# Decoder step on one core: the index stage loads x already turned and applies the row factors behind the projections

## The chip, the cores and the metric

One Trainium2 chip, one core. The metric is the device time of one execution in microseconds, as the median of several runs. Engines are named as in the profile: PE is TensorE, DVE VectorE, ACT ScalarE, POOL GpSimd, SP SyncE. A queue such as SPq or ACTq is that engine's issue of transfers.

## The reference, cut to what matters

Layer 0 of a two-layer decoder is sparse attention with an indexer. 1024 prompt rows and 64 sample rows (8 sequences of 8 tokens) of width 1024 are normed and projected; the indexer's queries (8 heads of 64), its one key per row (64) and its 8 head weights are part of that projection.

```python
def _rms_norm(x, gain):
    y = xf * lax.rsqrt(jnp.mean(xf * xf, axis=-1, keepdims=True) + EPS)
    return (y * gain).astype(x.dtype)

# _att_project, from xn = _rms_norm(x, att_norm)
q, k, v, iq, ik, iw, gate = _split(xn @ w_in, ATT_SIZES)
ik = _rms_norm(ik, ik_gain)
iw = iw * (IDX_HEADS ** -0.5 * IDX_DIM ** -0.5)

# _indexer_topk
s = jnp.einsum('bthd,bld->bthl', iq, ik)
score = jnp.einsum('bth,bthl->btl', iw, jax.nn.relu(s))
score = jnp.where(admissible, score, -jnp.inf)
_, idx = lax.top_k(score, topk)          # topk = 256
```

For the prompt the keys are the prompt's own; for the sample they are 8192 cached keys and the 8 new ones. A row factor r = rsqrt(mean(x^2) + EPS) multiplies a whole row of x, so it can be taken out of a product: x @ w with the gain alone gives iq / r, ik / r and iw / r. ReLU lets a positive factor through, so the score needs iw times r^2. The norm of ik cancels r but for its EPS: it becomes rsqrt(mean(ik_raw^2) + EPS * (mean(x^2) + EPS)).

## The kernel before, in words

`build` runs stages one after the other, each a block that all engines leave together: `index_project` (L217), `sample_scores` (L606), `head_project`, the attention of the prompt, and then the sample's attention and the DeltaNet layer. The change touches the first two and the tile `xnT` that they leave to the rest. Everything is float32.

**Rows and tiles.** Nine row tiles of 128 rows: tile 0 holds the 64 sample rows, tiles 1 to 8 the prompt. `xnT` is x normed and turned: 128 partitions of the width, 8 slices of it, 64 + 1024 columns of rows. Tiles are worked in three trios.

**`index_project`.** SP loads row tiles into a ring of three (`x`), the gain as a broadcast tile `gx`, key weights `wk` (72 columns) and query weights `wq` (512 columns). For each tile ScalarE sums the squares (L451), GpSimd forms the row factor (`rms_x`: L342, L343), VectorE multiplies row, factor and gain (`norm_x`, L519), TensorE turns the tile in 8 transposes (`transposes_x`, L373), and ScalarE copies them out (`evac_x`, L458). Then `keys(n)` (L383) projects the tile to 64 key and 8 head weight columns. ScalarE takes them (`take_keys`: L464, L465, squares in L471), GpSimd forms the key's factor (`rms_ik`: L350, L351), VectorE norms the key (`norm_ik`, L527), TensorE turns it (`transpose_ik`, L392) and ScalarE copies it to `ikT` (L477, L478). `queries(r)` (L407) projects a trio's queries in four parts, which ScalarE copies out (`take_queries`, L485).

TensorE's order is: transposes and keys of trio 0, its queries, its key transposes, the page ids (L433); then the same for trio 1 and the scores of prompt blocks 2 to 4; then for trio 2 and the scores of blocks 5 to 7. `key_scores` (L418) is followed by ScalarE's ReLU of two heads at a time (`relus`, L493, two buffers) and VectorE's weighted sum (`add_parts`, L540 and L544). GpSimd gathers eight pages of sample keys at the end of its list (`gather_keys`, L600), after all factors.

**The search.** The threshold of the top 256 of a prompt row is found bit by bit (`prompt_topk`): each step counts the scores above a candidate for each block of a group (L118, which also writes its accumulator), and then settles the bit in two small operations, L135 and L137, each waiting for the one before. At a group's end `choose` marks the chosen keys (L144 to L151). The first group (blocks 2 and 3) has 32 steps and 2 choices, the second (blocks 4 to 7) 32 and 4. `TOPK_IN` tells which steps lie in which stage: four after the first scores, eleven between `norm_ik(7)` and `norm_ik(8)`, 29 in `sample_scores`.

**`sample_scores`.** 32 gathers of 128 pages of 16 keys go through a ring of eight; each is used in two steps of TensorE. Gather n + 8 is released by the second use of gather n, so GpSimd has a burst of eight and then a pause. TensorE turns the keys (L679), multiplies (L689) and sums the heads (L702); ScalarE copies and applies ReLU (L736, L743). VectorE waits for a small mask (`cmn`), runs 29 search steps, and adds the mask to the last columns at the end (L766).

## Time and profile before

| | |
|---|---|
| median of 3 runs | 1866.98 us (1861.58 to 1869.72) |
| span of the profiled execution | 1911.6 us, 26707 instructions |
| that execution's own time around its span | not shown by the page |
| PE, DVE, ACT, POOL busy | 91%, 67%, 40%, 27% of the span |
| mean granted TensorE clock | 0.966 |
| mean over the span, DMA | 207.37 MB, 108 GB/s |
| index stage | 0 to 165 us |
| sample scores | 165 to 258 us |

The page gives busy time by engine and by line, for one execution; a time in the trace is counted from the first instruction. A row of the timeline has its start, its length, engine, line, operation, output and inputs, and in brackets how long the engine was idle before it and what released it.

### The profile page before, as it was taken

To read this page: it belongs to the slowest core of one execution; us is meant where nothing else is said; L and a number is where in the kernel's file an instruction comes from. 1 tells how busy PE (TensorE), PEld (TensorE's weight loads), DVE (VectorE), ACT (ScalarE), POOL (GpSimd) and SP (SyncE) were. 2 spreads that over 40 slices of the span, in tenths; PEclk is the share of its full clock that TensorE was granted. 3 is DMA by queue.
4 is the path that set the end of the run, shared out by engine and by line. 5 is a ranking of instruction groups with operands and counts; after the bars stand their busy time and mean duration, and the time that the engine had idled before them with its cause. 6 is when DMAs were issued, how large, how long until landed. Compare 5 with 4: busy or idle time off the path is not lost. (4 is left out here: it accounts for less than half of the span.)

```text
span 1911.6 us, 26707 instructions
## 1 busy us (share of the span) xinstructions
PE 1733.9 (91%) x10053; PEld 994.6 (52%) x10053; DVE 1274.5 (67%) x2068; ACT 759.6 (40%) x1805; POOL 518.8 (27%) x588
## 2 busy tenths in 40 slices
PE   6888999999989999999989769989996878999997
PEld 5453444444445566664434334434434776777774
DVE  1389957899976799964885334535553576777671
ACT  3447778852224344322212222222211544655550
POOL 2121300100101111002117666767522502222320
PEclk9999999999999999999999979999998899999999
DMA  4125530110124112003215445445579445343220
GB/s 132 36 91 174 180 135 14 44 39 28 56 111 176 66 67 101 32 12 136 67 44 145 123 122 154 147 143 157 149 266 325 119 130 141 109 105 87 76 63 36
DMA packets 159447, 207.37 MB, mean 108 GB/s; under 512 B 45160, under 2 KB 109120, under 8 KB 159296
## 3 DMA queue, kind: packets, MB, share of 16 engines
q1 hardware_dynamic: 117336, 149.65, 23.7%
q0 software_dynamic: 16896, 50.35, 8.7%
q10 hardware_dynamic: 25088, 5.66, 1.5%
q8 instruction: 81, 1.33, 0.3%
q14 instruction: 46, 0.38, 0.1%
HBM read 161.89 MB, written 43.74 MB: 108 GB/s over the span
## 5 line engine op out<-in xcount | busy, mean ns | idle before, releaser
L930 PE MATMUL acc<-w_qg,xnT 128*128 128x512 f32 x384 | 169.1, 593 | 0.0
L2130 POOL DMA_INDIRECT home<-in_cache_v,rowidx x128 | 129.6, 1013 | 68.7 <-issue 35.7
L1147 DVE MAX8 top_v<-scores 128x8 f32<-128x4100 f32 x32 | 141.6, 4426 | 0.3
L1149 DVE FIND_INDEX8 top_i<-top_v,scores 128x8 uint32<-128x4100 f32 x32 | 141.5, 4423 | 0.0
L1151 DVE MATCH_REPLACE8 scores<-top_v,scores 128x4100 f32<-128x4100 f32 x32 | 141.2, 4413 | 0.0
L3450 PE MATMUL PY<-home,ogT_dn 128*128 128x512 f32 x288 | 133.6, 609 | 5.8 <-DVE y_t L3936 5.1
L1348 PE MATMUL ring<-w_out_att,ogT_blk 128*128 128x512 f32 x256 | 111.4, 593 | 2.8 <-DMA w_out_att<-in_att_w_out 1.7
L930 PEld LDWEIGHTS acc<-w_qg,xnT 128*128 128x128 f32 x384 | 71.1, 190 | 81.6 <-issue 81.5
L930 PE MATMUL acc<-w_kvq,xnT 128*128 128x512 f32 x256 | 111.4, 593 | 0.0
L2453 DVE SCALAR_TENSOR_TENSOR y_ch<-x_pad,conv_w,y_ch 128x1024 f32<-128x1024 f32 x72 | 92.5, 1285 | 2.6
L186 ACT ACTIVATE junk_topk_h<-key_mask,bs_cand 128x640 f32<-128x640 f32 (+1 forms) x88 | 86.1, 981 | 15.7 <-DVE bs_cand L196 10.8
L1381 ACT COPY pT_blk<-tp_blk 128x512 f32<-128x512 f32 (+3 forms) x96 | 43.2, 487 | 123.6 <-PE tp_blk L1318 123.4
L2374 ACT COPY scores<-tpk 128x512 f32<-128x512 f32 x64 | 37.0, 588 | 137.1 <-PE tpk L2176 81.5
L2267 PE MATMUL acc_ch<-xnT,S_s 128*128 128x512 f32 x176 | 86.4, 636 | 4.1 <-issue 3.9
L2267 PE MATMUL acc_ch<-xnT,weight_sums 128*128 128x512 f32 x176 | 82.9, 614 | 4.1 <-issue 4.0
L3450 PEld LDWEIGHTS PY<-home,ogT_dn 128*128 128x128 f32 x288 | 53.3, 195 | 62.2 <-issue 60.8
L1309 PE MATMUL ring<-kT,w_kvq 128*128 128x512 f32 (+3 forms) x192 | 74.5, 499 | 11.9 <-DVE w_kvq L1454 5.6
L1429 DVE CUSTOM_DVE_ANT_0 lm<-ring,key_mask,q_scale 128x128 f32<-128x128 f32 (+7 forms) x64 | 51.7, 814 | 47.9 <-PE ring L1309 47.3
L1348 PEld LDWEIGHTS ring<-w_out_att,ogT_blk 128*128 128x128 f32 x256 | 48.3, 190 | 62.6 <-issue 61.0
L930 PEld LDWEIGHTS acc<-w_kvq,xnT 128*128 128x128 f32 x256 | 48.5, 190 | 61.1 <-issue 61.1
L2267 PE MATMUL acc_ch<-w_out_s,weight_sums 128*128 128x512 f32 x176 | 79.4, 594 | 0.3 <-issue 0.3
L1277 POOL TENSOR_TENSOR w_kvq<-w_kvq 128x512 f32<-128x512 f32 x15 | 19.1, 1276 | 216.6 <-ACT w_kvq L1394 215.6
(535 smaller groups left out, 3586.0 us busy)
## 6 DMA issues: line engine op xcount, KB each, us to landing
S_s<-in_dn_w_in SPq DMA_DIRECT2D x24, 512.0 KB
qkv_d<-y_ch SPq DMA_DIRECT2D x24, 512.0 KB
qkv_t<-qkv_d SPq DMA_DIRECT2D x8, 1536.0 KB, 8.1
home<-in_dn_w_in SPq DMA_DIRECT2D x5, 2048.0 KB, 11.2
x<-in_x_all SPq DMA_DIRECT2D x9, 512.0 KB, 3.7
out_y_all<-y_t SPq DMA_DIRECT2D x9, 512.0 KB, 2.9
w_kvq<-in_att_w_in SPq DMA_DIRECT2D x2, 2048.0 KB, 7.8
w_qg<-in_att_w_in SPq DMA_DIRECT2D x2, 2048.0 KB, 12.6
```

The lines of the kernel that those rows point to most:

```text
L186: ins = act.activation(self.junk[:, a:a + w], self.block(i), ACT.Sign, bias=self.cand[:, s:s + 1].bitcast(F32), scale=-1.0, accum_out=self ...
L930: ins = pe.matmul(acc[rows(n), k % ACC, :], xnT[:, kk, cols(n)], w[:, kk, :], start=(kk == 0), stop=(kk == KT - 1))
L1147: link(dve.max(v, scores[:]))
L1149: dve.max_index(top_i[:, 8 * r:8 * r + 8], v, scores[:])
L1151: link(dve.match_replace(scores[:], v, scores[:], -3e38))
L1309: ins = pe.matmul(dst[:, a:a + w], q[:, i % 2, h, :], kT[:, h // GRP, a:a + w], start=True, stop=True)
L1348: ins = pe.matmul(dst[:, a:a + 512], ogT[:, h, :], wo[:, h, a:a + 512], start=(h == 0), stop=(h == H - 1))
L1429: dve.tensor_tensor_reduce(lm[:, hc % LR, 0:w], ring[:, at["l", hc] % 2, 0:w], key_mask[:, KM[i]:KM[i] + w], keep["q_scale"][:, i, h:h + 1 ...
L2130: pool.indirect_dma_start(vg[:, j % VR, c, :], None, cv, bass.IndirectOffsetOnAxis(ap=rowidx[:, c, query(j):query(j) + 1], axis=0)).then_i ...
L2267: ins = pe.matmul(dst, left[:, k, :], right[:, k, :], start=(first and k == 0), stop=(last and k == 3), skip_group_check=True)
L2453: ins = dve.scalar_tensor_tensor(out, src, tap, out, ALU.mult, ALU.add)
L3450: ins = pe.matmul(PY[:], ogT[:, h, :], wo[:, h, r * 512:(r + 1) * 512], start=(h == 0), stop=(h == H - 1))
```

## The change

- The host hands in `x_cols`, x turned, and the gain by columns. SP loads it by trios straight into `xnT`, the first trio in two halves, and the query weights in two halves; VectorE multiplies slices of a trio by the gain in place (`gains`). Transposes, norms and evictions of x are gone.
- The row tiles are still loaded, by ScalarE's queue, three at once at the start, only for the sum of squares.
- GpSimd forms the row factor, its square and EPS times the mean for each tile, and multiplies the head weights (`rms_x`, `rms_ik`). Key tiles have three buffers instead of two.
- TensorE: keys 0 and 1, queries 0, keys 2 to 5, key transposes 0 to 2, page ids, queries 1, keys 6 to 8, key transposes 3 to 5, early scores, queries 2, key transposes 6 to 8, late scores. GpSimd gathers between the factors of tile 5 and those of tile 6. VectorE norms keys 3 to 8 ahead of the early sums.
- The search runs 13 steps in the index stage, all between early and late sums, and 31 in the sample scores.
- The row factors go to DRAM and come back as a broadcast row of 1088 to all partitions, the first load of the sample scores; there GpSimd multiplies the eight slices of `xnT` by it, one behind every third gather.

```diff
-TOPK_IN = {"index": (0, 4), "index_late": (4, 15), "sample_scores": (15, 44), "heads": (34 + 32, len(SEARCH))}
+TOPK_IN = {"index": (0, 13), "sample_scores": (13, 44), "heads": (34 + 32, len(SEARCH))}
...
 # SP, index_project
+            sp.dma_start(xnT[:, 0:4, trio(0)], xv[:, 0:4, trio(0)]).then_inc(xt_in[0], 16)
+            sp.dma_start(gxc[:], d["att_norm_cols"]).then_inc(gxc_in, 16)
+            sp.dma_start(wk[:], wv[:, :, IK0:G0]).then_inc(wk_in, 16)
+            sp.dma_start(xnT[:, 4:8, trio(0)], xv[:, 4:8, trio(0)]).then_inc(xt_in[1], 16)
+            sp.dma_start(wq[:, :, 0:256], wv[:, :, IQ0:IQ0 + 256]).then_inc(wq_in[0], 16)
+            sp.dma_start(wq[:, :, 256:512], wv[:, :, IQ0 + 256:IK0]).then_inc(wq_in[1], 16)
             sp.dma_start(ident[:], d["c_ident"]).then_inc(const_in, 16)
+            sp.dma_start(xnT[:, :, trio(1)], xv[:, :, trio(1)]).then_inc(xt_in[2], 16)
...
+            sp.dma_start(xnT[:, :, trio(2)], xv[:, :, trio(2)]).then_inc(xt_in[3], 16)
+            sp.wait_ge(rsi_ok, 1)
...
+            sp.wait_ge(rsx_ok, NT)
+                sp.dma_start(d["rs_d"][:, 0:NS].rearrange("o p -> p o"), rsx[0:NS, 0, :]).then_inc(rs_out, 16)
+                sp.dma_start(d["rs_d"][:, NS:].rearrange("o (n p) -> p (o n)", p=P), rsx[:, 1:NT, :].rearrange("p n o -> p (n o)")).then_inc(rs_out, 16)
...
 # GpSimd
             def rms_x(n):
                 pool.wait_ge(ssx_ok, n + 1)
+                link(pool.tensor_scalar(msx[:, n, :], ssx[:, n, :], 1.0 / DM, EPS, ALU.mult, ALU.add))
+                pool.tensor_scalar(epsm[:, n, :], msx[:, n, :], EPS, None, ALU.mult)
+                link(pool.tensor_tensor(rsx[:, n, :], msx[:, n, :], mhalf[:], ALU.pow))
+                link(pool.tensor_tensor(rs2[:, n, :], rsx[:, n, :], rsx[:, n, :], ALU.mult))
+                pool.tensor_scalar(rs2[:, n, :], rs2[:, n, :], IH ** -0.5 * ID ** -0.5, None, ALU.mult).then_inc(rsx_ok, 1)
             def rms_ik(n):
+                pool.wait_ge(rsx_ok, n + 1)
+                pool.tensor_scalar(iw_nat[q, n, :], ikr[q, n % 3, ID:ID + IH], rs2[q, n, :], None, ALU.mult)
+                link(pool.tensor_scalar(msi[q, n, :], ssi[q, n, :], 1.0 / ID, None, ALU.mult))
+                link(pool.tensor_tensor(msi[q, n, :], msi[q, n, :], epsm[q, n, :], ALU.add))
+                pool.tensor_tensor(rsi[q, n, :], msi[q, n, :], mhalf[q, :], ALU.pow).then_inc(rsi_ok, 1)
...
+            for n in range(3, 6):
+                rms_x(n)
+                rms_ik(n)
             pool.wait_ge(idx_ok, 1)
             gather_keys(pool, d, keep, k_in, 0, RING)
+            for n in range(6, NT):
+                rms_x(n)
+                rms_ik(n)
...
 # TensorE
+            keys(0)
+            keys(1)
+            queries(0)
+            for n in range(2, 6):
+                keys(n)
+            for n in range(3):
+                transpose_ik(n)
...
 # ScalarE
+                act.activation(junk[:], x[:, n % XR, :], ACT.Square, accum_out=ssx[:, n, :]).then_inc(ssx_ok, 1)
+                if n + XR < NT:
+                    act.wait_ge(ssx_ok, n + 1)
+                    load(n + XR)
...
+            for n in range(XR):
+                load(n)
+            take_keys(0)
+            take_keys(1)
+            for g in range(4):
+                take_queries(0, g)
+                if g < 3:
+                    square_x(g)
...
 # VectorE
+            def gains(r):
+                    dve.tensor_scalar(xnT[:, k, trio(r)], xnT[:, k, trio(r)], gxc[:, k:k + 1], None, ALU.mult).then_inc(xg_ok, 1)
...
+            for n in range(3, NT):
+                norm_ik(n)
+            for i in EARLY:
+                add_parts(i)
+            topk(*TOPK_IN["index"])
+            for i in LATE:
+                add_parts(i)
...
 # sample_scores
         def _(sp):
+            sp.wait_ge(env["stores"]["rs_out"], 32)
+            sp.dma_start(keep["rs_row"][:], d["rs_d"].partition_broadcast(P)).then_inc(rs_in, 16)
             sp.dma_start(cmn[:], d["c_new_causal"]).then_inc(loads, 16)
...
                 gather_keys(pool, d, keep, k_in, n, n + 1)
+                if n % 3 == 2:
+                    k = (n - RING) // 3
+                    if k == 0:
+                        pool.wait_ge(rs_in, 16)
+                    pool.tensor_tensor(xnT[:, k, :], xnT[:, k, :], keep["rs_row"][:], ALU.mult)
```

## Rows read from the trace of the kernel before

**Rows 1.** Busy time by stretch: span and length; engines with counts; clock; DMA share; GB/s.

```profile
46.60:60.50 13.90, 9.51 (x77) 8.57 (x77) 6.86 (x22) 7.56 (x21) 3.18 (x6) 1.00 0.27 82
60.50:81.00 20.50, 20.50 (x67) 12.15 (x66) 1.68 (x3) 3.62 (x13) 3.65 (x7) 1.00 0.08 27
...
83.50:105.20 21.70, 16.00 (x80) 6.69 (x81) 18.55 (x36) 13.98 (x19) 0.00 (x0) 1.00 0.00 0
...
111.30:134.40 23.10, 21.50 (x70) 12.57 (x69) 19.73 (x76) 4.00 (x14) 8.65 (x11) 1.00 0.53 187
134.40:165.00 30.60, 23.84 (x96) 7.40 (x96) 28.47 (x51) 21.80 (x24) 0.00 (x0) 0.98 0.00 0
165.00:258.00 93.00, 85.32 (x688) 38.65 (x688) 81.39 (x218) 71.66 (x105) 23.52 (x24) 0.97 0.53 182
```

The engines in each row are PE, its weight loads, DVE, ACT and POOL.

**Rows 2.** Timeline of the index stage.

```profile
7.16 1.28 DVE L519 SCALAR_TENSOR_TENSOR x<-x,rsx,gx 128x1024 f32<-128x1024 f32 x1 [7.16 <-DMA gx<-in_att_norm_rows]
...
21.68 1.06 ACT L451 ACTIVATE junk_x<-x 128x1024 f32<-128x1024 f32 x1 [5.52 <-DMA x<-in_x_all]
...
24.37 3.69 PE L383 MATMUL ik_ps<-w_ik,xnT 128*128 128x72 f32 x16 [5.26 <-ACT xnT L458]
...
27.85 18.69 PE L407 MATMUL iq_key_score<-xnT,w_iq 128*128 128x320 f32 x64
...
103.06 0.70 ACT L493 ACTIVATE relu_parts<-iq_key_score 128x640 f32<-128x640 f32 x1 [0.22 <-DVE key_mask L544]
```

**Rows 3.** Timeline of DVE in the sample scores.

```profile
167.01 0.61 DVE L118 TENSOR_SCALAR_CACHE_REDUCE junk_topk_s<-key_mask,bs_cand 128x384 f32<-128x384 f32 x1 [2.13 <-DMA new_causal<-in_c_new_causal]
...
195.98 0.17 DVE L135 TENSOR_SCALAR bs_rej<-bs_cnt 128x2 int32<-128x2 f32 x1
...
196.38 0.61 DVE L118 TENSOR_SCALAR_CACHE_REDUCE junk_topk_s<-key_mask,bs_cand 128x384 f32<-128x384 f32 x1
...
205.07 0.82 DVE L118 TENSOR_SCALAR_CACHE_REDUCE junk_topk_s<-key_mask 128x640 f32<-128x640 f32 x1
...
251.64 0.16 DVE L137 SCALAR_TENSOR_TENSOR bs_cand<-bs_cand,bs_rej 128x4 int32<-128x4 int32 x1
...
257.44 0.16 DVE L766 TENSOR_TENSOR scores<-rps,new_causal 128x4 f32<-128x4 f32 x1 [5.64 <-PE rps L727]
```

**Rows 4.** DMA totals from 12 to 20 us.

```profile
DMA packets 2197, 2.79 MB, mean 349 GB/s; under 512 B 880, under 2 KB 1024, under 8 KB 2197
```

**Rows 5.** Lines of the index stage, shapes apart: busy us, mean ns | idle.

```profile
L383 PE MATMUL ik_ps<-w_ik,xnT 128*128 128x72 f32 x128 | 17.0, 292 | 5.7 <-ACT xnT L458 5.7
...
L351 POOL TENSOR_TENSOR rsi<-msi,mhalf 128x1 f32<-128x1 f32 x8 | 4.3, 544 | 0.7
...
L350 POOL TENSOR_SCALAR msi<-ssi 128x1 f32<-128x1 f32 x8 | 1.5, 192 | 53.4 <-ACT junk_ik L471 53.2
...
L540 DVE TENSOR_SCALAR key_mask<-relu_parts,iw_nat 128x320 f32<-128x320 f32 x2 | 0.7, 384 | 0.0
```

**Rows 6.** Busy time in stretches of 2 us around the first queries (granted clock third last).

```profile
24.00:26.00 2.00, 1.63 (x8) 1.63 (x8) 1.67 (x3) 0.32 (x1) 1.92 (x2) 0.50 0.00 0
...
30.00:32.00 2.00, 2.00 (x8) 1.44 (x7) 0.46 (x3) 1.09 (x9) 1.06 (x4) 0.91 0.00 0
```

**Rows 7.** Timeline where DVE and POOL meet: a later stage, and the sample scores.

```profile
222.61 0.94 POOL L600 DMA_INDIRECT kraw<-in_cache_idx_k,idx_page  x1 [0.30 <-issue]
223.15 0.39 DVE L135 TENSOR_SCALAR bs_rej<-bs_cnt 128x4 int32<-128x4 f32 x1
...
888.14 2.34 POOL L1638 TENSOR_TENSOR gz<-tanh_z,gain_o 128x1024 f32<-128x1024 f32 x1
888.28 3.29 DVE L1817 SCALAR_TENSOR_TENSOR dn_ahead<-dn_ahead,dn_rs 128x1024 f32<-128x1024 f32 x1 [0.52 <-POOL dn_rs L1632]
```

**Rows 8.** Timeline of POOL in the sample scores: the first gathers of two bursts.

```profile
176.72 0.94 POOL L600 DMA_INDIRECT kraw<-in_cache_idx_k,idx_page  x1 [52.50 <-PE tps L679]
...
198.51 1.56 POOL L600 DMA_INDIRECT kraw<-in_cache_idx_k,idx_page  x1 [10.98 <-PE tps L679]
```

More of the change, by code:

```diff
@@ new lines, in _ @@
+            keys(1)
+            queries(0)
+            for n in range(2, 6):
+                keys(n)
+            for n in range(3):
+                transpose_ik(n)
+            pe.wait_ge(ptf_ok, 1)
+            pe.matmul(kq[:, 2, 0:DB * NGI], e16[:], ptf[:], start=True, stop=True).then_inc(ptb_ok, 1)
+            queries(1)
+            for n in range(6, NT):
+                keys(n)
+            for n in range(3, 6):
+                transpose_ik(n)
+            pe.wait_ge(idx_ok, 1)
+            pe.wait_ge(iq_ok, 8)
@@ L442, in _, with load @@
+            pe.wait_ge(tp_evac, 6)
+            for i in EARLY:
+                key_scores(i)
+            queries(2)
+            for n in range(6, NT):
+                transpose_ik(n)
+            pe.wait_ge(iq_ok, 12)
+            pe.wait_ge(tp_evac, NT)
+            pe.wait_ge(zeroed, 1)
+            for i in LATE:
+                key_scores(i)
         @block.scalar
         def _(act):
+            def load(n):
+                act.dma_start(x[:, n % XR, :], d["x_all"][n * P:(n + 1) * P, :]).then_inc(x_in[n % XR], 16)
@@ L473, in evac_ik @@
             def evac_ik(n):
[L474 removed]
                 m = NS if n == 0 else P
[L476 to L485 removed]
+                act.wait_ge(tp_done, n + 1)
```

323 lines of the change are left out of this document (125 added, 198 removed).

## The prediction

> **What bounds the kernel now.** TensorE is busy for 91% of the span, but the change touches only the first 258 us, so I read those by stage [rows 1]. The index stage ends at 165 us and is a relay. Until 27.85 us TensorE waits for rows: the first norm starts when the broadcast gain has landed at 7.16, ScalarE stands until 21.68 for a row tile, so the third keys run at 24.37 and the first queries at 27.85 [rows 2]. From 46.6 to 60.5 it turns and projects three more tiles. From 83.5 to 105.2 and from 134.4 to 165 the score sums bound: VectorE is busy for 18.55 of 21.7 us and 28.47 of 30.6 [rows 1]. Between these, TensorE turns and projects the last trio until 111.3, and the third queries hide VectorE's search (19.73 busy of 23.1). The sample scores (165 to 258) hold TensorE for 85.32 of 93 us and VectorE for 81.39 [rows 1]. There TensorE ends last: VectorE's last search step ends soon after 251.64, and it idles for 5.64 us before its last sum at 257.44 [rows 3]. These 5.6 us are all the slack it has, and the forecast turns on them.
>
> The stages end at common borders: a stage is worth what its last engine says, and the next keeps what it gains. The profiled span is 1911.6 us, and no time of that execution around its span is shown; the median of the runs, 1866.98, is 2.3% less. I take the difference from the profile and put it on the median.
>
> **The change, part by part: index stage.** *Opening.* Gone: the gain rows (512 KB), the transposes, norms and evictions of x. Needed before the first queries: two halves of the turned trio (655 KB each), key weights (295 KB) and half of the query weights (1 MB), and beside them on ScalarE's queue three row tiles (1.5 MB) that nothing early needs: 4.2 MB. Full queues moved 2.79 MB in 8 us, 349 GB/s [rows 4]; 4.2 MB are then 12.1 us, and with the first bytes at 2 us and about 1 us to the semaphore the query weights land at 15. The second half of the trio, with all ahead of it (3.2 MB), lands near 12; its four gain multiplications, of the form of the score sum's first product, 384 ns at 320 columns [rows 5], end near 13.5. Keys of two tiles follow: eight tiles took 17.0 us, 2.1 each [rows 5], more at low clock: keys began at a granted clock of 0.50 (1.2 of 2.4 GHz) after TensorE had stood for 5.26 us [rows 2, 6]. I take the first queries at 17: minus 10.9 us. Bounds: 15, weights just landed and keys quick; 21, at 250 GB/s. Of the first queries a part ran at half clock until about 31 [rows 6]; now TensorE runs without a hole before them: minus 1.2 (nothing to 1.5).
>
> *Between first and second queries.* Before 13.9 us [rows 1]. After: keys of four tiles (7.6 to 8.4 by rows 5) and small transposes with the page ids (1.7, an estimate from the 2.5 between the second queries and 83.5): 9.3. Minus 4.6.
>
> *Around the early scores.* The last rectified block ends at 103.8 [rows 2], the third queries began at 111.3: 7.5 us now go, but the keys of that trio come back ahead of the early scores, 5.8. Minus 1.7.
>
> *GpSimd's queue, a new wait.* VectorE now norms all nine key tiles before its first score sum, and the last three need row factors that GpSimd forms only after eight gathers. With second queries from 43.8 and 5.2 us for each of their four parts, the sixth tile's squares end at 56 and its factors at 59; eight gathers of 0.94 us with 0.3 between [rows 8] last until 69; three tiles of nine small operations each, 192 ns or for the powers 544 ns [rows 5] with 80 ns between, and the norm, until 78.4. The sums could have begun at 74.6: the second queries' end, 64.7, the keys and 4.1 of small steps. ScalarE and TensorE hold two buffers each and queue behind. Plus 3.8 (nothing to 6).
>
> *At nothing.* The search: 13 steps, not 15, are now all beside the third queries: 22.5 us at 1.73 each (rows 3, below) against 23.1 of cover [rows 1]; a step more would show whole. The squares of the row tiles (1.06 us, rows 2) lie between evictions 5 us apart; the six later loads cost ScalarE some 0.5 us of issue there. Later gains: beside queries. SP's ten head weight transfers now wait for the first key factor (about 26) and are needed near 50. SP's store of 1,088 row factors leaves near 78 and is wanted at 150; the last key stores stand behind it, and no one waits for them. Were that cover gone, each is 2 to 3 us.
>
> Sum for the stage: -10.9 -1.2 -4.6 -1.7 +3.8 = **-14.6**; it ends near 150.4.
>
> **Sample scores.** Three things go onto VectorE. (1) The row factors' broadcast (557 KB) is issued ahead of the small mask load for which VectorE waits until 167.01 [rows 3]: at 349 GB/s plus 1.5. (2) Two search steps: 17 took from 167.01 to 196.38, 1.73 each: plus 3.45. (3) Eight multiplications of 128x1088 on GpSimd, one after every third gather. The nearest row is 2.34 us for 128x1024 [rows 7], so 2.5 us each. They hold VectorE up: an operation with two inputs in SBUF that takes 1.28 us at 7.16 [rows 2] took 3.29 when it began 0.14 us behind such a multiplication, and ended 1.09 us after it [rows 7]. The search's small operation L135 took 0.39 us, not 0.17, and ended with a gather [rows 3, 7]. Every search step has a pair of such small operations, L135 and L137; the long counts have one tensor input, and no row shows them held.
>
> So each multiplication stops the search at its next small pair. In the first group (steps of 1.73) it is met after 0.86 us on average and holds for 2.5 - 0.86 = 1.64. In the second (10 steps from 205.07 to 251.64, 4.66 each) it is met in 2.5/4.66 of cases and holds for 1.25: 0.67. Gathers start at 176.72 and 198.51 [rows 8], 11.5 and 33.3 us into the stage, and three with a multiplication take 6.4 us. So four fall in the first group (6.6), two in the choosing between the groups (8.7 us, nearly all two-input or short operations; 1.7 and 2.3), two in the second group (1.3): 11.9, less 0.5 where waits overlap. 1.5 + 3.45 + 11.4 - 5.6 of slack = **+10.8**. Bounds: nothing if they never hold it (4.95 is under the slack), and with 8 times 2.5 for 11.4, +19.4, if the counts are held too. I take the middle: rows 7 show small and two-input operations held and nothing else.
>
> The Trainium skill says (SBUF — State Buffer, Who interferes with whom) that the shared port pair is taken for a whole instruction, and that the form of tensor_scalar that also writes its accumulator stays outside. By that exemption the stage's sum is +10.8, without it +19.4; no row here decides it for a long multiplication beside a long count.
>
> Gathers 9 to 15 go out later, behind three multiplications; TensorE may be 1 us late, but has 9 until VectorE ends. What shows instead is the clock: TensorE stands for 10 us before the projections. After 5.26 us of standing it had half clock from 24.37 to about 31 [rows 2, 6], 3 us lost; I take half, plus 1.5 (nothing to 3).
>
> **Sum:** -14.6 + 10.8 + 1.5 = -2.3. Predicted 1864.7.
>
> **The rivals.** *A, the lock hides.* If GpSimd gives way, or its work falls beside counts, VectorE ends within its slack, and the stage grows by 2 at most. For it: most of a step is a count. Against it: 3.29 us [rows 7]. Time: -14.6 + 2 = -12.6, 1854.4. *B, a shorter relay.* The factors fit (no 3.8) and the weights land at once: index -19.5, net -7, 1860. *C, slower: the opening is bound by its loads.* Place: the query weights' first half. The turned rows come in pieces of 1280 bytes, and the row tiles take every second turn on the other queue. Price: at half the rate of rows 4, 175 GB/s, 4.2 MB are 24 us; first queries at 27 as before, -14.6 becomes -4.6: net +8, 1875. It decides from where the weights land after 24 us. Against it: 349 GB/s were moved with small pieces among them. That the change doesn't do what it says would be the same place: turned loads as late as the transposes.
>
> **How the numbers follow.** Forecast 0.55 (its own range 1857 to 1872), A 0.17, B 0.16, C 0.12. A measurement can tell about 0.5% (9.3 us) from no change. Beyond it lie most of A (0.13), a quarter of B (0.04) and the forecast's tail (0.02): faster 0.19. Half of C (0.06) and the forecast with held counts (0.03): slower 0.09. Same 0.72. The range, 1853 to 1876, reaches from A to C and leaves under 0.2 out.
>
> **What would show it.** First queries near 17 us; only keys and small transposes between first and second queries; VectorE's first score sum some 4 us after it could start, released by a key factor; the border near 150. Then L135 or L137 up to 2.5 us long beside GpSimd's multiplications, and TensorE, not VectorE, idle at the end of the sample scores. I am wrong if VectorE still idles there for microseconds (A), or if the first queries wait for weights beyond 21 us (C).

## The result, and the profile after

Beside each other on one chip the changed kernel takes 1877.63 us (median of 6 runs, 1871.19 to 1884.37) and the kernel before 1864.98 (6 runs, 1861.58 to 1869.72): a ratio of 1.0070, 95% interval 1.0051 to 1.0089. A second set gave 1.0066 (1.0042 to 1.0090). The change costs 12.7 us where a gain of 2.3 was forecast, and the result lies outside the range of 1853 to 1876. (Runs taken beside each other are a set. "Set 1860.76" behind a time below is the median of the kernel before in the same set.)

| | before | after |
|---|---|---|
| median | 1864.98 us | 1877.63 us |
| profiled execution, its span | 1911.6 | 1875.8 (its own time 1877.61) |
| TensorE's first queries | 27.85 | 17.12 |
| index stage ends (VectorE's last operation in it) | 164.9 | 153.3 |
| VectorE's last sum of the sample scores | 257.4 | 264.0 |
| first product of the heads | 258.3 | 264.9 |

The span of before, 1911.6, is no contradiction. In some sets both kernels take some 60 us more, nearly all between 1040 and 1300 us, and what makes it is not known: one chip has a set of each kind (1923.07 and 1863.32 us for the kernel before). So times are compared only with those of the kernel before in the same set, and profiles by stretches that end at the same instructions.

The opening, in the timeline of TensorE, answers to [rows 2] (start, length, engine, line, in brackets the idle time before and what ended it):

```profile
10.09 1.22 PE L373 MATMUL ik_ps<-w_ik,xnT 128*64 128x72 f32 x8 [10.09 <-DMA w_ik<-in_att_w_in]
12.31 5.01 PE L373 MATMUL ik_ps<-w_ik,xnT 128*64 128x72 f32 x24 [1.00 <-DVE xnT L526]
17.12 18.82 PE L397 MATMUL iq_key_score<-xnT,w_iq 128*128 128x320 f32 x64
35.78 7.26 PE L373 MATMUL ik_ps<-w_ik,xnT 128*128 128x72 f32 x64
...
44.69 5.75 PE L397 MATMUL iq_key_score<-xnT,w_iq 128*128 128x384 f32 x17
```

First queries at 17.12, and 8.8 us between the end of the first (35.94) and the second (44.69): close to the forecast, 17 and 9.3. The queries took 18.82 us, as before (18.69), so the 1.2 us for the clock were not there: in both kernels the first four products start 0.53 to 0.63 us apart, and the later ones 0.27. The timeline of VectorE around the early scores:

```profile
73.95 0.48 DVE L534 SCALAR_TENSOR_TENSOR ikk<-ik_raw,rsi,gik 128x64 f32<-128x64 f32 x2 [13.12 <-POOL rsi L349]
77.52 0.48 DVE L534 SCALAR_TENSOR_TENSOR ikk<-ik_raw,rsi,gik 128x64 f32<-128x64 f32 x2 [3.09 <-POOL rsi L349]
81.08 0.48 DVE L534 SCALAR_TENSOR_TENSOR ikk<-ik_raw,rsi,gik 128x64 f32<-128x64 f32 x2 [3.08 <-POOL rsi L349]
81.48 0.41 DVE L547 TENSOR_SCALAR key_mask<-relu_parts,iw_nat 128x384 f32<-128x384 f32 x1
```

The new wait is there, the three last norms behind GpSimd's factors. They come 3.57 us apart, where nine operations at the forecast's prices are 3.15, and the first sum starts at 81.5, not 78.4.

In the sample scores VectorE now ends last. Its timeline (answers to [rows 3]), and GpSimd's at two of these places:

```profile
158.69 0.61 DVE L118 TENSOR_SCALAR_CACHE_REDUCE junk_topk_s<-key_mask,bs_cand 128x384 f32<-128x384 f32 x1 [5.45 <-DMA new_causal<-in_c_new_causal]
...
166.90 2.38 DVE L135 TENSOR_SCALAR bs_rej<-bs_cnt 128x2 int32<-128x2 f32 x1
...
172.56 2.89 DVE L135 TENSOR_SCALAR bs_rej<-bs_cnt 128x2 int32<-128x2 f32 x1
...
178.72 2.87 DVE L135 TENSOR_SCALAR bs_rej<-bs_cnt 128x2 int32<-128x2 f32 x1
...
264.03 0.16 DVE L776 TENSOR_TENSOR scores<-rps,new_causal 128x4 f32<-128x4 f32 x1
```

```profile
171.95 0.94 POOL L603 DMA_INDIRECT kraw<-in_cache_idx_k,idx_page  x1 [0.30 <-issue]
172.91 2.50 POOL L678 TENSOR_TENSOR xnT<-xnT,rs_row 128x1088 f32<-128x1088 f32 x1
175.57 0.98 POOL L603 DMA_INDIRECT kraw<-in_cache_idx_k,idx_page  x1 [0.16 <-PE tps L689]
...
178.09 0.94 POOL L603 DMA_INDIRECT kraw<-in_cache_idx_k,idx_page  x1 [0.30 <-issue]
179.05 2.50 POOL L678 TENSOR_TENSOR xnT<-xnT,rs_row 128x1088 f32<-128x1088 f32 x1
```

L135 starts at 172.56, inside the gather, and ends at 175.45, in the gap of 0.16 us behind the multiplication. Time that an operation takes beyond its own, because GpSimd is at work, is called a hold here. There are eight, six of 2.2 to 2.8 us and two of 0.5 and 1.5, in all 17.8 us above the 0.17 that such an operation takes alone. TensorE waits too, for gathers that leave late. Its waits for gathers from 153.4 to 251 us (total, times, longest), and the busy times there and from 251 to 264.9 (answer to [rows 1]):

```profile
PE tps L689 <- DMA kraw<-in_cache_idx_k,idx_page: 6.8, 8, 2.2
```

```profile
153.40:251.00 97.60, 88.30 (x688) 38.97 (x688) 88.92 (x202) 73.10 (x105) 43.03 (x32) 0.95 0.53 179
251.00:264.90 13.90, 0.02 (x2) 0.05 (x2) 12.78 (x29) 0.00 (x0) 0.21 (x5) 0.54 0.00 0
```

(Columns: stretch, its length, busy us of TensorE's matmuls and weight loads, VectorE, ScalarE, GpSimd, the granted clock, DMA share, GB/s.) In the last 13.9 us VectorE works alone.

### The profile page after: what moved, and what is told of

Same layout as the page of the kernel before. It is cut to its first block and busy times, and to the rows that moved or that the text cites. A ratio compares the mean times of both kernels' runs of the same rounds, so it can differ in the third digit from the quotient of the medians.

```text
span 1875.8 us, 26591 instructions
## 1 busy us (share of the span) xinstructions
PE 1722.0 (92%) x9981; PEld 986.5 (53%) x9981; DVE 1288.2 (69%) x2083; ACT 752.0 (40%) x1778; POOL 545.8 (29%) x641
## 5 line engine op out<-in xcount | busy, mean ns | idle before, releaser
L940 PEld LDWEIGHTS acc<-w_qg,xnT 128*128 128x128 f32 x384 | 71.1, 190 | 81.6 <-issue 81.5
L186 ACT ACTIVATE junk_topk_h<-key_mask,bs_cand 128x640 f32<-128x640 f32 (+1 forms) x88 | 86.1, 981 | 29.0 <-issue 18.4
L1319 PE MATMUL ring<-kT,w_kvq 128*128 128x512 f32 (+3 forms) x192 | 75.0, 502 | 12.5 <-PEq L784 6.1
L1287 POOL TENSOR_TENSOR w_kvq<-w_kvq 128x512 f32<-128x512 f32 x15 | 19.1, 1275 | 217.7 <-ACT w_kvq L1404 216.7
L2277 PE MATMUL acc_ch<-xnT,S_s 128*128 128x512 f32 x176 | 81.9, 609 | 0.0
## 6 DMA issues: line engine op xcount, KB each, us to landing
home<-in_dn_w_in SPq DMA_DIRECT2D x5, 2048.0 KB, 10.9
```

The lines of the kernel that those rows point to most:

```text
L186: ins = act.activation(self.junk[:, a:a + w], self.block(i), ACT.Sign, bias=self.cand[:, s:s + 1].bitcast(F32), scale=-1.0, accum_out=self ...
L940: ins = pe.matmul(acc[rows(n), k % ACC, :], xnT[:, kk, cols(n)], w[:, kk, :], start=(kk == 0), stop=(kk == KT - 1))
L1319: ins = pe.matmul(dst[:, a:a + w], q[:, i % 2, h, :], kT[:, h // GRP, a:a + w], start=True, stop=True)
L2277: ins = pe.matmul(dst, left[:, k, :], right[:, k, :], start=(first and k == 0), stop=(last and k == 3), skip_group_check=True)
```

## The experiments

**The kernel before again, twice, and the changed kernel again, twice.** No edit. The forecast rests on one profile of before.

> The kernel before once more, for a second profile of it. The profiled execution that stands in the front part took 1911.6 us of span against 1866.98 us of the median; aligned by instruction, it loses some 45 us between 1040 and 1300 us and nothing before. Expected: a span within 0.5% of 1865 us, and up to 280 us the same times as the first profile within 1 us (index stage ends at 164.9, VectorE's last addition of the sample scores at 257.4).

> The changed kernel once more, for a second profile and a tighter time. Against the second profile of the kernel before, its first profile stands 6.9 us behind at 280 us, 8.7 at 600, 9.2 at 1100, and 17.5 to 18.8 from 1560 us to the end. If the last 8 us are a cost of the change, the second profile has them too; if they are the state of TensorE's clock where the scan begins, the two profiles differ there by several us. Expected: 6.5 to 7.5 us behind at 280 us, as the holds of VectorE repeat, and a time 9 to 15 us above the kernel before.

> The kernel before once more, beside the changed one on the same chip, for the stretch behind 1440 us. If the changed kernel loses there by its order or its streams, this profile runs level with the other profiles of the kernel before (within 2 us of each other from 1440 to 1850) and the changed kernel's falls behind it by 6 us or more; if it is the clock's chance, this one falls behind its own kind by as much.

> The changed kernel on the same chip as the profile of the kernel before beside it. By the theory of the holds it stands 5 to 8 us behind at 280 us; by the losses seen so far 7 to 10 us behind at 1000 us; and if the loss behind 1440 us belongs to the change, 6 us more at the end.

| profile | index stage ends | VectorE's last sum | heads' first product | holds |
|---|---|---|---|---|
| before, first | 164.9 | 257.4 | 258.3 | 0.5 |
| before, second (e0) | 170.3 | 257.0 | 257.8 | 0.4 |
| before, third (e11) | 170.7 | 262.3 | 263.1 | 0.4 |
| after, first | 153.3 | 264.0 | 264.9 | 17.8 |
| after, second (e7) | 153.5 | 261.5 | 262.4 | 15.5 |
| after, third (e12) | 153.5 | 261.9 | 262.7 | 15.5 |

The expectation of e0 was missed: the kernel before varies by 6 us in the index stage and by 5 at the heads, the changed one by 0.2 and 2.5. The index stage varies with TensorE's clock. From 54.6 to 68.3 us, in the first profile of before, in e0 and in the first profile of the changed kernel (columns as above, the granted clock third last):

```profile
54.60:68.30 13.70, 12.38 (x64) 9.14 (x65) 3.35 (x6) 6.48 (x23) 6.28 (x11) 1.00 0.18 59
```

```profile
54.60:68.30 13.70, 13.13 (x48) 11.04 (x49) 3.35 (x6) 5.71 (x20) 6.77 (x12) 0.50 0.15 49
```

```profile
54.60:68.30 13.70, 13.70 (x62) 9.20 (x60) 1.02 (x5) 4.42 (x11) 9.21 (x17) 1.00 0.60 171
```

In e0 TensorE ran at half clock for the second trio's products and into its queries, and the third queries began at 116.81 instead of 111.42. e11 has the same (0.52), the changed kernel's profiles do not (1.00 in all three). VectorE's slack varies too. The 5.64 us of the first profile are 5.06 in e11 and nothing in e0, where TensorE ended at 256.58 and the last sum follows VectorE's own last step:

```profile
256.96 0.16 DVE L766 TENSOR_TENSOR scores<-rps,new_causal 128x4 f32<-128x4 f32 x1
```

In the mean the changed kernel starts the heads at 263.3, the kernel before at 259.7: 3.6 us of the 12.7 are lost by then. The time of e7 was as expected (9 to 15 us above), but at 280 us it stood 4.9 us behind e0, not 6.5 to 7.5. The expectation of e12 was missed: beside e11 it was 0.7 us ahead at 280 us, 0.3 behind at 1000 and 1.9 behind at the end. That of e11 was missed in part. Its scan is level with its own kind (the stretches below), but from 1700 to 1850 us it lost 8.6 us against e0, 7.3 of them behind 1780, where its clock was granted 0.50 twice for 6.8 us. That hides the scan's 8.5 us between e11 and e12 at the end. The times of e0, 1859.41 us (set 1860.76), and of e11 and e12, 1930.57 and 1932.33 (set 1923.07), are single runs.

**Without the multiplications (e1).** The projections of the heads then lack the row factor of x.

```diff
-                if n % 3 == 2:
...
-                    pool.tensor_tensor(xnT[:, k, :], xnT[:, k, :], keep["rs_row"][:], ALU.mult)
```

> The changed kernel without GpSimd's eight multiplications of 2.50 us (it leaves out the row factor of x for the projections of the heads). Theory (the multiplications hold VectorE's search: eight waits of 0.64 to 2.99 us, 15.8 us in all): the waits go, VectorE's last addition of the sample scores comes at 247 to 250 us instead of 264.0, with TensorE's scores as the bound or level with it, and the time falls by 13 to 17 us, to 1861 to 1865 us. Rival (the two search steps more and the late mask load are what costs, and the holds are noise in a search that waits anyhow): the addition stays at 260 us or later and the time within 5 us of 1877.6.

The last sum is at 246.4, with no hold, and the ratio to before is 0.9983 (0.9962 to 1.0003), 16 us under the changed kernel. TensorE's part of the sample scores fell from 97.0 us to 86.8, its 6.8 us of waits for gathers gone; the rest is no more than that part varies by (91.9, 85.8 and 90.9 us in the three profiles of before). TensorE ended at 240.6, so VectorE still set the end, where the expectation had the two level. Its chain from the index stage's end to the last sum is 93.2 us against 86.7 in e0, which is the late mask and the two steps. So the eight multiplications are most of what made the stage long, on both engines.

**All eight behind the last gather (e4).**

```diff
-                if n % 3 == 2:
-                    k = (n - RING) // 3
-                    if k == 0:
-                        pool.wait_ge(rs_in, 16)
-                    pool.tensor_tensor(xnT[:, k, :], xnT[:, k, :], keep["rs_row"][:], ALU.mult)
+            pool.wait_ge(rs_in, 16)
+            for k in range(KT):
+                pool.tensor_tensor(xnT[:, k, :], xnT[:, k, :], keep["rs_row"][:], ALU.mult)
```

> The changed kernel with all eight multiplications behind the last gather instead of one behind every third. Theory (each hold is the alignment of one short operation of the search with a gather and the multiplication right behind it, 15.8 us in all; and every multiplication delays the next gathers, for which TensorE waits 6.8 us): in a row, each multiplication of 2.5 us stretches one search step of 1.72 us to 2.5 us, 8 x 0.8 = 6.4 us and up to 2.5 us for the first, so 7 to 9 us instead of 15.8, TensorE ends 4 to 6 us earlier than at 250.8, and VectorE's last addition comes 7 to 9 us earlier than 264.0; the time falls by 6 to 9 us. Rival (the multiplications take a fixed toll of the search, 2 us each, wherever they stand): VectorE's waits stay at 14 to 17 us and the addition within 2 us of 264.0.

The ratio is 1.0074 (1.0046 to 1.0102): no gain. TensorE ended at 241.3, 9 us earlier, where the theory had 4 to 6. But VectorE's last sum stayed at 264.5; there the rival had the size, by another mechanism. The timelines of VectorE and GpSimd:

```profile
217.61 1.28 DVE L118 TENSOR_SCALAR_CACHE_REDUCE junk_topk_s<-key_mask,bs_cand 128x1024 f32<-128x1024 f32 x1
218.93 17.43 DVE L135 TENSOR_SCALAR bs_rej<-bs_cnt 128x4 int32<-128x4 f32 x1
236.40 0.16 DVE L137 SCALAR_TENSOR_TENSOR bs_cand<-bs_cand,bs_rej 128x4 int32<-128x4 int32 x1
```

```profile
216.64 19.70 POOL L676 TENSOR_TENSOR xnT<-xnT,rs_row 128x1088 f32<-128x1088 f32 x8
```

One hold of 17.4 us, which ends when GpSimd's row does, at 236.34. Between multiplications that follow without a gap VectorE's operation doesn't get in. The theory had given it a turn behind each.

**The same multiplications, paced (e10).** GpSimd begins each when the search's chain has counted the end of a step: two tiles in halves, beside steps of the first group (1.4 us of counts), six whole, beside steps of the second (4.3 us).

```diff
+        PACED = {15: [(i // 2, halves[i % 2], first + 3 * (13 + i)) for i in range(4)],
+                 23: [(2 + i, whole, pairs + 4 * (1 + i)) for i in range(2)],
+                 31: [(4 + i, whole, pairs + 4 * (6 + i)) for i in range(4)]}
...
+                    pool.wait_ge(env["topk_chain"]["sem"], done)
+                    pool.tensor_tensor(xnT[:, k, part], xnT[:, k, part], keep["rs_row"][:, part], ALU.mult)
```

> The changed kernel with the same eight multiplications on GpSimd, but each begun when the search's chain says that a step has just ended: four halves of 544 columns behind gather 16, two whole ones behind gather 24, four behind the last gather (two tiles as halves, six whole). Theory (what holds VectorE is one short operation of the search arriving inside an unbroken run of GpSimd work, until that run ends; it is not the multiplications' share of time, nor their number): a whole one of 2.5 us fits into the 4.3 us of long operations of a step of the second group, a half one of 1.25 us into the 1.4 us of the first group, so the holds fall from 15.5 to 17.8 us to under 4, VectorE's last addition comes at 247 to 251 us instead of 261.6 to 264.2, and the time is 10 to 15 us less than the changed kernel's, ratio to the kernel before 0.997 to 1.001. Rival (GpSimd's multiplications take their time from VectorE wherever they fall): the holds show up in the long operations or behind them, and the addition stays at 260 us or later.

GpSimd, and VectorE beside it:

```profile
205.66 2.52 POOL L683 TENSOR_TENSOR xnT<-xnT,rs_row 128x1088 f32<-128x1088 f32 x1 [5.61 <-DVE bs_cand L131]
```

```profile
205.62 0.88 DVE L118 TENSOR_SCALAR_CACHE_REDUCE junk_topk_s<-key_mask,bs_cand 128x640 f32<-128x640 f32 x1
206.42 1.01 DVE L118 TENSOR_SCALAR_CACHE_REDUCE junk_topk_s<-key_mask,bs_cand 128x768 f32<-128x768 f32 x1
207.35 1.14 DVE L118 TENSOR_SCALAR_CACHE_REDUCE junk_topk_s<-key_mask,bs_cand 128x896 f32<-128x896 f32 x1
208.54 1.28 DVE L118 TENSOR_SCALAR_CACHE_REDUCE junk_topk_s<-key_mask,bs_cand 128x1024 f32<-128x1024 f32 x1
209.86 0.17 DVE L135 TENSOR_SCALAR bs_rej<-bs_cnt 128x4 int32<-128x4 f32 x1
...
248.97 0.16 DVE L781 TENSOR_TENSOR scores<-rps,new_causal 128x4 f32<-128x4 f32 x1 [1.56 <-PE rps L742]
```

All the arithmetic is there, and no operation of the search is held by more than 0.3 us. The counts beside a multiplication are as long (0.88, 1.01) as those of the next step without one. The last sum, at 249.0, waits for TensorE again. The ratio is 0.9995 (0.9970 to 1.0021). This shows the mechanism: not the load, but a short operation that arrives inside an unbroken run of GpSimd's work.

**Three small parts (e2, e3, e6), one run each.** The first asks for the mask ahead of the row factors.

```diff
+            sp.dma_start(cmn[:], d["c_new_causal"]).then_inc(loads, 16)
             sp.wait_ge(env["stores"]["rs_out"], 32)
             sp.dma_start(keep["rs_row"][:], d["rs_d"].partition_broadcast(P)).then_inc(rs_in, 16)
-            sp.dma_start(cmn[:], d["c_new_causal"]).then_inc(loads, 16)
```

> The changed kernel with the load of the 4-column mask asked for ahead of the row factors' load (544 KB to all partitions) and of the wait for the factors' store. Theory: VectorE's search starts 3 to 4 us earlier (it began at 158.7 with a wait of 5.45 us for that load), and as VectorE sets the end of the sample scores, its last addition comes 2 to 4 us earlier than 264.0, unless the shift brings more of the search's short operations under GpSimd's multiplications (1 to 2 us either way). Rival (TensorE sets the end of the stage): the addition stays at 264.0 within 1 us and shows idle time behind TensorE.

The search starts 2.9 us into the stage instead of 5.5, and the last sum is at 262.5 (1872.30 us; set 1860.76). The late mask costs about 2.5 us, of which holds of 18.0 us left little. The second puts the gathers behind the last factors.

```diff
-            pool.wait_ge(idx_ok, 1)
-            gather_keys(pool, d, keep, k_in, 0, RING)
             for n in range(6, NT):
                 rms_x(n)
                 rms_ik(n)
+            pool.wait_ge(idx_ok, 1)
+            gather_keys(pool, d, keep, k_in, 0, RING)
```

> The changed kernel with GpSimd's first eight gathers behind the factors of the last three tiles instead of ahead of them. Theory: the factors of tiles 6 to 8, which come at 73.9, 77.5 and 81.1 us behind gathers that end at 70.4, come 10 us earlier, VectorE begins the early sums at 74 to 76 us instead of 81.5, the early scores end 5 to 6 us earlier, and the index stage ends at 147 to 149 us instead of 153.7; the gathers still land long before the sample scores. Rival (TensorE or ScalarE hold the early scores then): the stage ends less than 2 us earlier.

The first early sum starts at 78.0 and the index stage ends at 150.3: 3 us earlier, not 5 to 6. VectorE still waits for factors: with the gathers out of the way GpSimd waits 6.93 us for ScalarE's squares of tile 6. Most of the 3 us is gone by the last sum (261.7; 1932.37 us, set 1922.99): the holds come to 18.4. The third moves two search steps back.

```diff
-TOPK_IN = {"index": (0, 13), "sample_scores": (13, 44), ...
+TOPK_IN = {"index": (0, 15), "sample_scores": (15, 44), ...
```

> The changed kernel with 15 search steps in the index stage and 29 in the sample scores, as the kernel before has it, instead of 13 and 31. Theory: two steps of 1.72 us leave the sample scores, where VectorE sets the end, and enter the index stage, where VectorE waits for TensorE by less than that: the index stage ends 2 to 3.5 us later, the sample scores take 3.5 us less, and the sum is within 1.5 us of no change, up to one hold of 2.7 us either way. Rival (the move of the two steps is what made the sample scores longer): VectorE's last addition comes 3 us or more earlier than 264.0.

The index stage ends 2.4 us later (155.8), the last sum is at 262.9 (1938.63 us, set 1928.02). Moving the two steps is a wash.

**Natural rows later (e5).**

```diff
-            for n in range(XR):
-                load(n)
             take_keys(0)
             take_keys(1)
+            for n in range(XR):
+                load(n)
```

> The changed kernel with ScalarE's three first loads of rows in natural layout (512 KB each) asked for behind its copies of the first two tiles' keys instead of at once. Theory: in the opening 2.8 MB of rows, turned x and weights share the DMA engines at some 350 GB/s; without 1.5 MB of rows ahead of them the second half of x, the key weights and the query weights land 3 to 4 us earlier, the first queries begin at 13 to 14 us instead of 17.1, and all up to the end of the early scores follows by as much, unless the squares of the rows then come too late for the norms of tiles 0 to 2. Rival (the opening waits for its own loads' latency): the first queries begin within 1 us of 17.1.

First queries at 13.5, 3.7 us earlier than in e7; the index stage ends at 150.4. The rows were in the way of the opening, as expected. At the last sum 0.7 us is left (260.8), with holds of 17.8. Its time, 1923.47 us (set 1928.02), is a single run and lower than its stretches account for.

**The row factor in ScalarE's copies (f1), and without its scratch tensor (f1b).** ScalarE scales by the row's factor where it copies the heads' projections out; the multiplications, the factors' store and broadcast go. Not in the lines shown: the sample rows are loaded twice, so that their factors stand in both halves of the partitions.

```diff
-                    act.copy(v_nat[q, n, :], src[:, 256:512])
+                    act.mul(v_nat[q, n, :], src[:, 256:512], f)
...
-                act.activation(sgate[:, 0, 0:512], acc[:, k % ACC, :], ACT.Silu).then_inc(acc_rd, 1)
+                act.activation(sgate[:, 0, 0:512], acc[:, k % ACC, :], ACT.Silu, scale=keep["rsx"][:, 0, :]).then_inc(acc_rd, 1)
```

> The changed kernel with the row factor of x taken into ScalarE's copies out of PSUM in the projections of the heads (scale by the row's factor), instead of GpSimd's eight multiplications; the factors' store and the load to all partitions go too. Theory: the search is held by nothing and the mask no longer waits behind 544 KB, so VectorE's last addition comes 3 to 4 us earlier than in the kernel without multiplications (246.4), at 242 to 244 us, and the time is 2 to 5 us less than that kernel's 1858.4, so 8 to 3 us below the kernel before. Rival (ScalarE's copies with a scale by the row take longer, and ScalarE is what the projections wait for): the gain at 247 us is given back by 530 us.

> The same as the kernel with the factor in the copies, with the scratch tensor of the row factors (4352 bytes in DRAM, unused there) taken out, so that every DRAM tensor behind it lies where it lay before. All changed kernels lose 7 to 9 us against the kernel before between 1440 and 1850 us, where the code is the same and short transfers to and from DRAM stand in the chain. Theory (their addresses matter): this kernel is 4 to 8 us faster than the one with the tensor, all of it behind 1440 us. Rival (the clock's dips fall otherwise): the two are within 2 us.

Ratios 0.9982 (0.9962 to 1.0002) and 0.9982 (0.9960 to 1.0004). The last sum is at 249.5 and 248.0, not 242 to 244, and TensorE sets it again. Two things made it later: the index stage ended at 158.0 and 156.0, with first queries at 18.7 and 18.9 (probably the second load of the sample rows, which nothing tests), and TensorE's part took 90.8 and 91.3 us instead of e1's 86.8. The scratch tensor's place in DRAM made no difference to the time, so DRAM addresses are out as the cause of the later loss.

**All of it (f3): factor in the copies, gathers last, rows late.**

> The kernel with the row factor in ScalarE's copies, with the first eight gathers behind the factors of tiles 6 to 8 (3 us earlier early sums in the run that has this alone), and with the natural rows asked for behind the first keys. Theory: the gains add, as TensorE now sets the end of the sample scores and its start follows the index stage: the index stage ends at 147 to 149 us, the sample scores at 240 to 243, and the time is 5 to 7 us below that of the kernel with the factor in the copies alone, ratio to the kernel before 0.993 to 0.996. Rival (the first gathers, now later, or the rows, now later, take their place): ratio within 0.001 of 0.998.

The ratio is **0.9924** (0.9896 to 0.9952), faster than both kernels. The index stage ends at 147.9, the heads begin at 240.3. Freed of the holds, both small parts keep their gain.

**72 transposes more on TensorE (f4 from f3, e13 from the changed kernel), and 36 and 144 (e14, e15 from f3).**

```diff
+            pe.wait_ge(const_in, 16)
+            for _ in range(72):
+                pe.transpose(tpb[0:32, 0, 3, 0:32], ident[0:32, 0:32], ident[0:32, 0:32])
             for n in range(3):
                 transpose_ik(n)
```

> The same kernel with 72 more transposes of 32 x 32 on TensorE (their output is not used), placed where TensorE waits for the norms of tiles 0 to 2: it makes TensorE's instruction stream as long as that of the kernel before, which had 72 transposes of x. All changed kernels lose 6 to 9 us against the kernel before between 1440 and 1850 us in code that is the same; in each of them TensorE's queue stands for 2.4 to 3.1 us without a wait at the second group of products of the state (u with k_masked) at 1507 to 1529 us, where the kernel before has 1.6 us or none. Theory (where the stream lies relative to its loading decides): that stall is gone here and the kernel is 2 to 5 us faster than its twin behind 1440 us. Rival: the stall stays and the two lie within 2 us.

> The changed kernel as it is, with 72 transposes of 32 x 32 on TensorE more (output unused) where TensorE waits for the norms of tiles 0 to 2; they took 2.3 us there. Four profiles of changed kernels at a time show the same in the stretch of the scan that the three profiles of the kernel before pass in 139.8 to 140.2 us (1560 to 1700): 142.8 to 147.7 us, with 2.9 to 6.0 us in 4 or 5 stalls of TensorE without a wait against 0.3 to 0.6 us in one; and 61 to 67 us against 59.9 to 60.7 in the 60 us ahead of it. The one kernel with 72 transposes added has 140.1 and 60.7 us and one stall. Theory (taking 72 transposes out of TensorE's stream shifted where its loading falls in the scan's code): here too 60 to 61 us and 140 to 141 us, and a time 4 to 8 us below the changed kernel's, ratio to the kernel before 1.002 to 1.005. Rival (what the one kernel showed was chance, or its other edits): 143 to 146 us and the ratio at 1.0066 to 1.0074.

> The kernel with the factor in the copies, the gathers last and the rows late (its scan stretches: 64.1 and 142.8 us), with 36 transposes added instead of 72. If the position of the stream decides, the stalls fall on other instructions than with none or with 72: the two stretches come out between 200 and 209 us in sum, by where they fall, and the lines with stalls differ from those of both. If each added transpose helps by itself, the sum lies midway, at 203 to 204 us, with fewer stalls than with none on the same lines.

> The same with 144 transposes. If the position decides, twice the number that was right is not right again: stalls of 2 us or more in sum in the stretch of 140 us, which takes 142 us or more. If more instructions help by themselves: 140 us and at most one stall, as with 72.

The stretches of the scan, between the same products of TensorE, from the kernel before (e0), the changed one (first profile) and e13, one fence each:

```profile
1500.00:1559.90 59.90, 54.28 (x595) 45.62 (x595) 43.46 (x134) 29.54 (x68) 9.15 (x13) 0.90 0.63 186
1559.90:1700.10 140.20, 137.98 (x1891) 105.02 (x1890) 103.32 (x284) 83.21 (x236) 40.13 (x58) 1.00 0.34 90
```

```profile
1509.60:1574.30 64.70, 55.88 (x595) 46.20 (x594) 43.54 (x134) 29.26 (x68) 9.68 (x13) 0.88 0.59 172
1574.30:1718.70 144.40, 138.59 (x1891) 105.50 (x1891) 103.94 (x289) 83.36 (x236) 39.34 (x58) 1.00 0.33 88
```

```profile
1518.10:1576.80 58.70, 52.81 (x596) 44.45 (x595) 42.58 (x133) 29.39 (x68) 7.76 (x11) 0.92 0.65 189
1576.80:1717.40 140.60, 137.84 (x1892) 105.08 (x1891) 104.47 (x284) 83.28 (x236) 41.33 (x60) 1.00 0.34 90
```

The same 1891 products, the same clock in the second stretch, and 4.2 us more. TensorE stands there without a wait, in the timeline of the changed kernel at five places, in e0's at one:

```profile
1578.91 0.31 PE L3318 MATMUL PA<-T,Y 32*32 32x32 f32 x11 [1.30 <-issue]
1618.64 1.05 PE L3441 MATMUL PB<-u,k_decay 128*128 128x128 f32 x7 [0.88 <-issue]
1656.15 0.61 PE L3312 MATMUL PA<-Y,T 32*32 32x32 f32 x49 [0.31 <-issue]
1659.53 0.63 PE L3327 MATMUL PA<-T,decay 32*32 32x32 f32 x28 [0.91 <-issue]
1699.04 0.44 PE L3327 MATMUL PA<-T,decay 32*32 32x32 f32 x16 [0.90 <-issue]
```

```profile
1565.80 0.24 PE L3317 MATMUL PA<-T,decay 32*32 32x32 f32 x2 [0.58 <-issue]
```

| | both stretches, us |
|---|---|
| before, three profiles | 200.4, 200.1, 200.6 |
| after, three profiles | 209.1, 208.1, 209.1 |
| the other ten without added transposes | 203.8 to 213.3 |
| f3; with 36; with 72 (f4); with 144 | 206.9; 207.8; **200.8**; 211.0 |
| e13: after with 72 | **199.3** |

Putting back as many transposes as the change took out gives the old stretches, twice; half or double that number doesn't (e14 has four stalls, all at one line, 4.3 us in sum; e15 four, 3.8 us). In all thirteen profiles without added transposes the first stall of the second stretch is at the same instruction line, L3318 of the changed kernel. So it goes by where the code stands in TensorE's stream, not by more instructions being better, and is hardly chance. That the stalls are late loads of code is argued only: the profile's instruction queue moved 81 packets (1.33 MB) before, 80 in the changed kernel and 81 in f4 and e13, but also 81 in e15, which stalls.

The time of e13 did not fall, ratio 1.0076 (1.0056 to 1.0096), and that expectation was missed: behind the added transposes the second queries began 4.9 us later (49.55) and in part at half clock (0.50 from 45.9 to 52.7 us), the index stage ended 6.9 us later (160.3), and the holds grew to 18.2, and to 20.4 with one of L150 in `choose`, 3.00 us for 0.75. Against the first profile of the changed kernel it lost 9.3 us until the heads had begun (280 us) and won 9.8 in the scan. f4 has a ratio of **0.9901** (0.9865 to 0.9937), against f3's 0.9924: the intervals overlap. e14 and e15 took 1852.72 and 1863.85 us in single runs (set 1863.32).

## Why the prediction was wrong

Two terms account for most of every timed kernel. "Heads" is the first product of the heads against 259.7, the mean of the three profiles of before; "scan" is the two stretches above against 200.4; "measured" is the ratio less one, times the median of before in that set.

| kernel | heads | scan | sum | measured |
|---|---|---|---|---|
| after (means; two sets) | +3.6 | +8.4 | +12.0 | +13.1, +12.7 |
| e1 no multiplications | -12.5 | +7.0 | -5.5 | -3.2 |
| e4 at the end | +5.7 | +11.2 | +16.9 | +13.8 |
| e10 paced | -9.8 | +3.4 | -6.4 | -1.0 |
| f1, f1b | -9.3, -10.9 | +5.0, +8.6 | -4.3, -2.3 | -3.5, -3.5 |
| f3 | -19.5 | +6.5 | -13.0 | -14.7 |
| f4 | -17.8 | +0.4 | -17.4 | -19.1 |
| e13 | +14.8 | -1.1 | +13.7 | +14.2 |

The sums rest on single profiles and the measured values on intervals of 4 to 7 us either way; they agree within 6. That is a check of the sizes, not a full account: the stretches between and behind the two vary as well (see Open).

**Right.** The opening (17.12 for 17), the 8.8 us between the queries (forecast 9.3), and the place and kind of the new wait on GpSimd. The index stage gained 11.6 us against the profile read, where 14.6 was forecast. Against the mean of three it gained 15.2, but that agreement is luck: two of the three have the half clock from 54.6 to 68.3 us, which the forecast did not know of. The small operations are what is held, and the counts are not. There the rule of the Trainium skill that I set the sum by (SBUF — State Buffer, Who interferes with whom: the form that writes its accumulator stays outside) agrees with the trace (counts of 0.88 and 1.01 us beside a multiplication in e10). The same section's "whole instruction", which the prediction takes over, is too short for e4: there one operation was held through eight multiplications. TensorE stood idle at the end of the stage, as said. Rivals A, B and C fell: the holds don't hide, the factors' wait was there, and the loads were not late.

**Mis-sized: the sum "1.5 + 3.45 + 11.4 - 5.6 of slack".** For the holds, 11.4, the runs have 17.8, 15.5 and 15.5. The prediction took the mean wait over all phases, 1.64 us. But the search and the gathers fall into step: gather, gather, gather with a multiplication repeats every 6.2 us; a hold of 2.7 and two steps of 1.72 fill that, and the third step's short operation meets the next gather. It meets the gather ahead of the multiplication and so waits for all of it: 2.7 to 2.8 us five times in the first profile, and near the mean once. The mask cost 3.2 us in the mean (a wait of 5.45, 5.09 and 5.47 for 2.1) instead of 1.5. And "5.6 us are all the slack it has" was one profile's: 5.6, 0 and 5.1, 3.6 in the mean. In the mean the sample scores with the step to the heads took 109.9 us against 91.1: +18.8, not +10.8. Of the 8.0 us more, the three terms give 4.9, 1.7 and 2.0, 0.6 too much.

**Small.** The factors cost 6.4 us instead of 3.8 (the gathers until 70.4 and 3.57 us a tile); the clock gave nothing in the opening and cost nothing extra at the heads. There the granted clock was 0.50 in the first 4.2 us (264.9 to 269.1), but before, without the idle time, it was 0.59 (258.3 to 262.5). "TensorE may be 1 us late" was 6.8 us of waits, still under VectorE.

**Missing: "a stage is worth what its last engine says, and the next keeps what it gains".** This step failed outright. The sum ended at the heads. The scan, 1200 us later and untouched, takes 8.4 us more because 72 transposes left TensorE's stream. The prediction counted them as time saved and not as a shift of all the code behind them. The sample scores and the scan, 8.0 and 8.4 us, less 0.6 that the index stage gained beyond its forecast and 1.5 charged for a clock loss at the heads that didn't come, are 14.3 of the 15.0 us of the miss, by the means of three profiles.

**Open.** Why TensorE's stream stalls where it does, and so which counts are good; in the second stretch the stalls, 4.3 us against 0.6, are 3.7 of the 4.2 us lost; in the first they come to 3.9 us against 2.3, 1.6 of its 4.8. Waits for VectorE add 1.6 there (4.9 against 3.3), and the same 595 products were busy for 1.6 us longer, at a clock of 0.88 against 0.90. Outside the two terms: from 280 to 1040 us all changed kernels but e7 lose 1.0 to 5.5 us against e0, where the other two profiles of before stand at -0.1 and 1.3. From 1040 to 1500 they differ by -2.7 to 6.3 from the profiles of before of the same kind of set. Behind 1780 us e1, e7, e10, e13 and f3 lose 3 us and e11 7.3, each time with the granted clock at 0.50 for 6.8 us where the others have 1.00. None of this was followed.

## What to carry to other kernels

Work for GpSimd that is put beside a chain of short VectorE operations costs by where it starts, not by how much it is. Start it from the chain's own count, or fold it into a copy that another engine makes anyway; spread out with gaps (the changed kernel) or in one block (e4) it cost about the same. Ask of a mean wait whether the two rhythms can lock. When instructions leave an engine's stream, look at engine stalls without a wait far behind the change before calling later code untouched, and read a border or a slack that varies by 5 us from more than one profile.

## What the runs showed of the hardware

- A short VectorE operation of 0.17 us took 17.43 when it met eight multiplications in a row on GpSimd, and ended with the last of them. In the changed kernel a gap of 0.16 us between two of GpSimd's instructions let it through.
- A gather (0.94 us on GpSimd) begins such a run: a hold that started inside it lasted through the multiplication behind it (L135 at 172.56: 2.89 us). Alone a gather cost 0.2 us or so (0.39 and 0.42 for 0.17).
- The same 1891 products of TensorE took 139.8 to 140.6 us or 142.8 to 147.7, by how many TensorE instructions stood 1500 us ahead of them.
